# Attention with alternating score pairs, its coefficient on GpSimd, and the output projection begun between the last tiles

## The reference, cut to what matters

```python
def block(qi):
    s = jnp.einsum('bqhmd,bkhmd->bhmqk', qi, k) * scale
    p = jax.nn.softmax(s, axis=-1)
    pd = p[:, :, 0] - lam * p[:, :, 1]
    return jnp.einsum('bhqk,bkhv->bqhv', pd.astype(v.dtype), v)
...
o = _rmsnorm(o, p['subln_g'][l]) * (1.0 - lam_init)
mix = jnp.concatenate([o.reshape(B, S, D_ATTN), rg], axis=-1) @ p['w_out'][l]
```

## Time and profile before

| what | value |
| --- | --- |
| median of three runs | 2250.62 us |
| profiled execution | 2247.88 us, span 2246.1 us |
| TensorE busy | 2166.9 us, 96% of the span |
| VectorE busy | 1552.5 us, 69% |
| ScalarE busy | 834.0 us, 37% |
| GpSimd busy | 47.2 us, 2% |
| attention, first pair of tile 2 to first pair of tile 35 | 1144.97 to 1314.96 us |
| mean granted TensorE clock | 0.991 |

### The profile page before, as it was taken

The page is one execution under the profiler, slowest core; times in us unless marked ns, Lnnn a source line. Parts: engine busy times, 40 slices in busy tenths (PEclk is TensorE's granted clock), DMA queues, the critical chain, the costliest instruction groups (busy, mean ns, idle before and its releaser), DMA issues.

```text
span 2246.1 us, 34066 instructions
## 1 busy us (share of the span) xinstructions
PE 2166.9 (96%) x13144; PEld 2103.6 (94%) x13144; DVE 1552.5 (69%) x2580; ACT 834.0 (37%) x1503; POOL 47.2 (2%) x79
## 2 busy tenths in 40 slices
PE   5999999999999999999989989999999999999997
PEld 4989999999999999899977879899999999999996
DVE  6977777777878775675768874686454547756556
ACT  5622232334212143655267762353232323411122
POOL 0000000000000000000011030000000000000000
PEclk8999999999999999999999999999999999999999
...
## 3 DMA queue, kind: packets, MB, share of 16 engines
...
...
## 4 chain that ended last, share of the span: by engine, by line
PE 89%; DVE 7%; ACT 2%; issue 1%; DMA 1%; SPq 0%; DVEq 0%; ACTq 0%
PE ps L786 16%; PE ps L788 16%; PE ps L787 16%; PE ps L861 9%; PE ps L862 9%; PE ps L863 9%; PE ps L1041 7%; PE ps L1172 2%; DVE sb_nmx L2415 1%; PE ps L1023 1%; PE ps L1117 1%; DMA sb_stage<-in_w_mod 1%; PE ps L1158 1%; PE ps L1125 1%; ACT sb_pr L1677 1%
## 5 line engine op out<-in xcount | busy, mean ns | idle before, releaser
L786 PE MATMUL ps<-sb_hH,sb_wH 128*128 128x384 f32 x1664 | 563.3, 339 | 8.0 <-DVE sb_wL L1906 3.7
L787 PE MATMUL ps<-sb_hL,sb_wH 128*128 128x384 f32 x1664 | 557.9, 335 | 0.0
L788 PE MATMUL ps<-sb_hH,sb_wL 128*128 128x384 f32 x1664 | 557.7, 335 | 0.0
L786 PEld LDWEIGHTS ps<-sb_hH,sb_wH 128*128 128x128 f32 x1664 | 313.9, 189 | 15.2 <-DVE sb_wL L1906 4.4
L787 PEld LDWEIGHTS ps<-sb_hL,sb_wH 128*128 128x128 f32 x1664 | 313.7, 188 | 1.2 <-issue 0.3
L788 PEld LDWEIGHTS ps<-sb_hH,sb_wL 128*128 128x128 f32 x1664 | 313.7, 189 | 0.0
L2180 DVE SCALAR_TENSOR_TENSOR sb_x<-ps,sb_mod,sb_x 128x384 f32<-128x384 f32 (+2 forms) x384 | 186.3, 514 | 172.7 <-PE ps L788 167.4
L861 PE MATMUL ps<-sb_hH,sb_wH 128*128 128x384 f32 x704 | 236.1, 335 | 4.2 <-DVE sb_tmp L2040 3.9
L862 PE MATMUL ps<-sb_hL,sb_wH 128*128 128x384 f32 x704 | 235.9, 335 | 0.0
L863 PE MATMUL ps<-sb_hH,sb_wL 128*128 128x384 f32 x704 | 235.8, 335 | 0.0
L1326 ACT ACTIVATE sb_wH<-sb_wide 128x512 fp32r<-128x512 f32 x176 | 110.9, 633 | 228.8 <-DVE sb_wide L1924 223.7
...
## 6 DMA issues: line engine op xcount, KB each, us to landing
...
```

The lines of the kernel that those rows point to most:

```text
L786: pe.matmul(o, wH, xH, start=begin, stop=False)
L787: pe.matmul(o, wH, xL, start=False, stop=False)
L788: return pe.matmul(o, wL, xH, start=False, stop=end)
```

## The change

Five things are done.

1. The order of the scores of a latent tile: three stacked for m = 0 as before; then three times a pair followed by one stacked matmul for m = 1. The signal that map 0 is complete is still given by the third pair's matmul for m = 0.
2. The coefficient of the difference is computed on GpSimd (`coefficient`, one multiplication by two per-partition scalars). VectorE only makes the reciprocal of the second sum, at the start of the next turn and ahead of the maxima, and the difference waits for `coef_ready`. All 36 coefficients stand in GpSimd's list ahead of the 27 multiplications of the attended tiles.
3. ScalarE no longer scales the attended tile by the reciprocal of the first sum. The norm absorbs it: before the roots, VectorE adds the squared sum times 128 times epsilon (`add_floor`).
4. `SPLIT_AT` has five entries instead of six, later ones; the sixth piece of work (queries of head 1) is done ahead of the loop. Of the three last value matmul groups one moves to turn 0 and two stay in turn 1.
5. At the end, the high parts of the operand tiles of chunk 0 are made in turns 35, 36 and 37 (`MIX_AT`) and the matmuls of `first_mix` stand between the groups of turns 37 and 38.

The core of the diff (left out: declarations and renamed semaphores):

```diff
-MIX_ORDERS = ((0, 1, 2, 4, 5, 6, 7, 3), (4, 5, 6, 7, 0, 1, 2, 3), (4, 5, 6, 7, 0, 1, 2, 3))
+MIX_ORDERS = ((4, 5, 0, 1, 2, 6, 7, 3), (4, 5, 6, 7, 0, 1, 2, 3), (4, 5, 6, 7, 0, 1, 2, 3))
 MIX_ORDER = MIX_ORDERS[1]
-SPLIT_AT = {1: (1, 0), 3: (1, 1), 5: (2, 0), 7: (2, 1), 11: (3, 0), 13: (3, 1)}
+MIX_AT = {TILES - 1: (4, 5), TILES: (0, 1, 2), TILES + 1: (6, 7)}
+SPLIT_AT = {4: (1, 1), 8: (2, 0), 10: (2, 1), 17: (3, 0), 20: (3, 1)}
...
-            sums = sb("sums", [P, 3, 2], F32, s)
-            rec = sb("rec", [P, 6, 2], F32, s)
+            sums = sb("sums", [P, TILES, 2], F32, s)
+            floor = sb("floor", [P, TILES], F32, s)
+            rec = sb("rec", [P, 3], F32, s)
...
-            for hd in range(NH):
-                stack_queries(hd)
-                stack_keys(hd)
+            def coefficient(u):
+
+                r = u % 3
+                pool.wait_ge(coef_ready, 2 * u + 1)
+                pool.tensor_scalar(coef[:, r:r + 1], rec[:, r:r + 1], sums[:, u, 0:1], nlam[:, 0:1], ALU.mult,
+                                   ALU.mult).then_inc(coef_ready, 1)
+
+            stack_queries(0)
+            stack_keys(0)
+            pool.wait_ge(small_in, 3)
+            for u in range(TILES):
+                coefficient(u)
+                if u == 2:
+                    stack_queries(1)
+                elif u in SPLIT_AT:
+                    hd, is_k = SPLIT_AT[u]
+                    (stack_keys if is_k else stack_queries)(hd)
             pool.wait_ge(o_rec, 1)
...
+            def stacked_scores(u, m, begin, spans=range(3)):
 
                 hd, q = u // QT, u % QT
-                for p in range(3):
+                for p in spans:
                     mm = pe.matmul(ps[:, 3 * m + p, 0:CH], queries(hd)[:, m, (q - 1) * P:q * P],
                                    keys_of(hd)[:, m, p * CH:(p + 1) * CH], start=begin, stop=not begin)
                 return mm
...
                 pe.wait_ge(e_done, 2 * u)
                 for p in range(3):
                     mm = low_scores(u, 0, p, False)
+                    if p == 2:
+                        mm.then_inc(s_ready, 1)
                     low_scores(u, 1, p, True)
+                    mm = stacked_scores(u, 1, False, (p,))
                 mm.then_inc(s_ready, 1)
-                stacked_scores(u, 1, False).then_inc(s_ready, 1)
 
             def group(u, g):
 
@@ -1173,16 +1192,30 @@
                     if k == nk - 1:
                         m.then_inc(o_ready, 1)
 
+            def first_mix(f, ks, begin, end):
+                if begin:
+                    pe.wait_ge(raw_used[f], used_wo[f] + 2)
+                for k in ks:
+                    pe.wait_ge(mix_lo, mixed(0, k))
+                    m = three(ps[:, f * NC, 0:CH], wiH[:, f, k * P:(k + 1) * P], wiL[:, f, k * P:(k + 1) * P],
+                              hv(hH, 0, k), hv(hL, 0, k), begin and k == ks[0], end)
+                if end:
+                    m.then_inc(w_ready, 1)
+
             pe.wait_ge(m_ev, 6 + 48)
             pe.wait_ge(acst, N_ACST)
             pe.wait_ge(roped, 1)
-            pe.wait_ge(v_ev, 15)
+            pe.wait_ge(v_ev, 13)
             for u in range(TILES + 3):
+                if u == 1:
+                    pe.wait_ge(v_ev, 15)
                 if u < TILES:
                     scores(u)
-                if u == 1:
-                    for n in range(15, 18):
-                        v_last(n)
+                if u == 0:
+                    v_last(15)
+                elif u == 1:
+                    v_last(16)
+                    v_last(17)
                 elif u == 2:
                     pe.wait_ge(v_ev, 18)
                 for g in range(3):
@@ -1190,9 +1223,16 @@
                         group(u - 2, g)
                     if g < 2 and 0 <= u - 3 < TILES:
                         values(u - 3, g)
+                    if u == TILES + 1 and g < 2:
+                        first_mix(0, (4 + g,), g == 0, False)
                 if u == TILES:
                     for hd in range(NH - 1):
                         outputs(0, hd)
+                elif u == TILES + 1:
+                    first_mix(1, (4, 5), True, False)
+                    first_mix(0, (0, 1, 2), False, False)
+                elif u == TILES + 2:
+                    first_mix(1, (0, 1, 2), False, False)
 
             def out_chunk(i, c, between=None):
 
...
-                pe.wait_ge(raw_used[f], used_wo[f] + 2)
-                first_mix(f, MIX_ORDERS[0][:KT - 1], True, False)
+                first_mix(f, (6, 7), False, False)
...
+                elif n == 12:
+                    qk_high(1, 0)
...
                 if u < TILES:
                     act.wait_ge(mx_ready, 2 * u + m + 1)
                     act.activation(by_bank(probs(u, m)) if u % QT else probs(u, m), unit(u, m), ACT.Exp,
-                                   bias=nmx[:, u % 2, m:m + 1], accum_out=sums[:, u % 3, m:m + 1]).then_inc(e_done, 1)
+                                   bias=nmx[:, u % 2, m:m + 1], accum_out=sums[:, u, m:m + 1]).then_inc(e_done, 1)
 
             def out_squares(u):
 
                 hd, t = u // QT, u % QT
                 act.wait_ge(o_ready, u + 1)
                 act.wait_ge(o_ss, u + 1)
-                act.activation(tmp[:, 3, 0:P], ps[:, 7, 0:P], ACT.Square, scale=rec[:, u % 6, 0:1],
+                act.activation(tmp[:, 3, 0:P], ps[:, 7, 0:P], ACT.Square,
                                accum_out=ss[:, hd, t:t + 1]).then_inc(o_ss, 1)
                 if u == QT:
                     act.wait_ge(outs, 48)
-                act.activation(attended(hd, t), ps[:, 7, 0:P], ACT.Copy, scale=rec[:, u % 6, 0:1]).then_inc(o_done, 1)
+                act.activation(attended(hd, t), ps[:, 7, 0:P], ACT.Copy).then_inc(o_done, 1)
 
             def roots_of_outputs(h0_, h1):
 
-                act.wait_ge(o_ss, 1 + h1 * 9)
-                act.activation(ss[:, h0_:h1], ss[:, h0_:h1], ACT.Sqrt, bias=eps[:, 0:1], scale=1.0 / P).then_inc(o_sd, 1)
+                act.wait_ge(o_floor, h1 // NH + 1)
+                act.activation(ss[:, h0_:h1], ss[:, h0_:h1], ACT.Sqrt, scale=1.0 / P).then_inc(o_sd, 1)
 
             def mix_high(c, k):
 
-                if (c, k) == (0, 0):
+                if (c, k) == (0, 4):
+                    act.wait_ge(t_ready, groups_before(TILES - 2))
+                elif (c, k) == (0, 6):
                     act.wait_ge(t_ready, groups_before(TILES - 1))
                 elif (c, k) == (1, 4):
                     act.wait_ge(o_done, TILES)
@@ -1710,17 +1743,16 @@
                 p_copy(u - 2, 0)
                 exps(u, 0)
                 exps(u, 1)
-                if u == 1:
-                    for n in range(15, 18):
+                if u < 2:
+                    for n in ((15,), (16, 17))[u]:
                         v_evac(n)
                 if u in SPLIT_AT:
                     qk_high(*SPLIT_AT[u])
                 p_copy(u - 2, 2)
                 if 3 <= u < TILES + 3:
                     out_squares(u - 3)
-                if u == TILES:
-                    for k in MIX_ORDERS[0][:KT - 1]:
-                        mix_high(0, k)
+                for k in MIX_AT.get(u, ()):
+                    mix_high(0, k)
                 if u == (NH - 1) * QT + 4:
                     roots_of_outputs(0, NH - 1)
                 if (NH - 1) * QT + 5 <= u < (NH - 1) * QT + 7:
...
                 dve.tensor_reduce(nmx[:, u % 2, m:m + 1], unit(u, m), AX.XY if u % QT else AX.X, ALU.max,
                                   negate=True).then_inc(mx_ready, 1)
 
-            def difference(u):
+            def add_floor(h0_, h1):
+
+                at = slice(h0_ * QT, h1 * QT)
+                dve.wait_ge(o_ss, 1 + h1 * QT)
+                link(dve.scalar_tensor_tensor(floor[:, at], sums[:, at, 0], P * EPS, sums[:, at, 0], ALU.mult, ALU.mult))
+                dve.tensor_tensor(ssf[:, at], ssf[:, at], floor[:, at], ALU.add).then_inc(o_floor, 1)
+
+            def reciprocal(u):
 
                 r = u % 3
                 dve.wait_ge(e_done, 2 * u + 2)
-                link(dve.reciprocal(rec[:, u % 6], sums[:, r]))
-                link(dve.scalar_tensor_tensor(coef[:, r:r + 1], sums[:, r, 0:1], nlam[:, 0:1],
-                                              rec[:, u % 6, 1:2], ALU.mult, ALU.mult))
-                dve.scalar_tensor_tensor(probs(u, 0), probs(u, 1), coef[:, r:r + 1], probs(u, 0), ALU.mult,
+                dve.reciprocal(rec[:, r:r + 1], sums[:, u, 1:2]).then_inc(coef_ready, 1)
+
+            def difference(u):
+
+                dve.wait_ge(coef_ready, 2 * u + 2)
+                dve.scalar_tensor_tensor(probs(u, 0), probs(u, 1), coef[:, u % 3:u % 3 + 1], probs(u, 0), ALU.mult,
                                          ALU.add).then_inc(pd_ready, 1)
 
             def p_copy(u):
@@ -2443,6 +2485,8 @@
                 m.then_inc(mix_lo, 1)
 
             for u in range(TILES + 3):
+                if 1 <= u <= TILES:
```

(15 more changed lines are left out.)

24 lines of the change are left out of this document (9 added, 15 removed).

## The result

The kernel with the change takes **2290.76 us**, the median of four executions (2286.25 to 2293.82). The kernel before takes 2249.42 us. The ratio is 1.0186, with a 95% interval of 1.0161 to 1.0211: it is 1.9% slower, just under the 2% that the prediction named as what tells from no change, with the interval's upper end just above it. One execution of the kernel before (2699.86 us) and one of e7 (4677.85 us) lie far outside all others and count in no ratio. The forecast was 2276 us, within 2256 to 2292.

A forecast was written before the change was run, and what follows sets the result against it. A loop over TensorE, VectorE and ScalarE bounds each latent tile at 4.97 us. Terms 24.8 + 2.5 + 1.2 - 2.2 + 0 = +26.3 on 2247.9 gave 2274 us profiled, 2277 median; stated 2276, range 2256 to 2292.

The forecast's parts named there:

- No change beyond 2%: Whole kernel: the time stays within 2% (45 us) of before, 2205.6 to 2295.6 us; chance 0.90.
- The lone piece: Scores on TensorE: a pair or stacked matmul alone between two mode changes takes 0.38 us, bounds 0.17 and 0.44.
- The loop: Latent tile over three engines: first pair to maxima grows from 0.83 to 2.00 us, the tile from 4.97 to 6.14.
- the rival that VectorE is the true bound: Latent tiles: VectorE's own list sets the pace, 4.70 us a tile, 2235 us in all; chance 0.05.
- The rival of a free change: Scores on TensorE: alternating mode changes cost nothing, 5.32 us a tile, 2254 us in all; chance 0.10.
- TensorE's own 0.83: Scores of a latent tile: TensorE's own work grows by 0.83 us to 5.80 a tile, within 6.14.
- Coefficient, low parts, tables: Attention loop: moved coefficient worth nothing, low parts hidden; ScalarE's two table loads ahead of tile 32 cost 0.8 us.
- Context tiles, +2.5: Steps around the three context tiles: TensorE works without pause, so its 0.83 us counts each time, +2.5 us.
- The other 27 steps: Steps between latent tiles, tile 2 to tile 35: 27 x 6.14 plus 0.8 for tables against 141.8, +24.8 us.
- The start, -2.2: Start of the attention: value matmuls of turn 0 fill TensorE's gaps and the clock may stay up, -2.2 us (-3.6 to +1).
- The clock: Attention: TensorE's clock falls to its lower level, up to 1.7 us each, past 2% from 11 falls; chance 0.06.
- The end, 0: Attention's end and first output chunk: 3 to 4 us won, as much lost waiting for GpSimd; 0 (-4 to +5).

The follow-up runs named there:

- e7: Kernel before with one stacked matmul of map 1 moved behind the first pair, one alternation instead of two: 2267.85 us, ratio 1.0076.
- e1: Kernel before with only the new order of the scores: 2285.06 us, ratio 1.0165.
- e6: Kernel before with the third pair's matmul for map 1 split off behind one stacked matmul, map 0 complete as early as before: 2263.71 us, ratio 1.0067.
- e2: Changed kernel with the old order of the scores, the rest of the change kept: 2249.35 us, ratio 1.0004.
- e9: Changed kernel run once more without any edit: 2288.16 us, ratio 1.0177 to the kernel before.
- e11: e5 with twelve matmuls that nobody reads added in turn 2: 2239.12 us, ratio 0.9956 to the kernel before.
- e10: e4 with twelve more matmuls that nobody reads in turn 2: 2284.34 us, ratio 1.0159 to the kernel before.
- e4: Changed kernel with nine matmuls that nobody reads ahead of each context tile's values: 2285.01 us, ratio 1.0169 to the kernel before.
- e8: Changed kernel, new order kept, with GpSimd's nine multiplications of chunk 0 moved behind the coefficients of tiles 32 to 34: 2284.98 us, ratio 1.0166.
- e5: Changed kernel with the old order and GpSimd's nine multiplications of chunk 0 moved behind the coefficients of tiles 32 to 34: 2241.66 us, ratio 0.9970.

## Why the prediction was right

**No change beyond 2%, and the range: both held, both narrowly; the number was 15 us low.** In the profiled execution the forecast was 2247.9 + 26.3 = 2274.2 us and 2293.82 were measured, 19.6 more. The median of 2290.76 lies 1.2 us below the upper end of the range. That end was made of a lone piece of 0.44 us and an end of +5, which did not come; the clock, which the range was said to leave out in the main, used up their room. The mechanism of the loop was right, but that the range held is in part luck. Of the signs named for a wrong forecast one came, a clock below 1.00 in the middle of the attention; the others (starts 0.17 apart, a tile below 5.5 us, differences waiting for GpSimd) did not.

**The lone piece, 0.38 us: right.** 0.37 to 0.38 from start to start in the after profile, in e1 and in e7. That 0.10 lies on each side of a change was read from two neighbours in the earlier trace rows; e6 and e7, which add one alternation in two different places, both give 0.57 for it, that is 0.20 for each change added to the 0.17 of the matmul.

The weight load of a lone pair in the after profile:

```profile
1178.97 0.19 PEld L1142 LDWEIGHTS ps<-sb_kstack,sb_qk_rest 64*128 64x128 f32 x2 [0.19 <-issue]
```

**The loop, 0.83 to 2.00 and the tile 4.97 to 6.14: right.** 1.97, and 6.11 to 6.12. The rest of the loop, 2.66 + 1.48, did not move by 0.01. e2 excludes the rival that VectorE is the true bound: relieved of its 0.45 us it idles 0.48. The rival of a free change falls with every start in the alternation. Nor is a weight load pulled ahead across a change: in the row above it starts with its matmuls, at 1178.97, after the weight loads have stood idle for 0.19 us, and those of the stacked matmuls on either side do the same; the load of the transposes behind them, in one mode with its neighbour, starts at 1180.23, 0.15 us ahead of its matmul. The Trainium skill, "TensorE: Matmul & The Clock Gate", section "The mechanism", which says that a load aimed at the background buffer is pulled ahead of running matmuls, is not borne out in this place. With its page "TensorEngine Tiling (Array Packing)", section "Key Properties", by which a change of the tiling mode drains TensorE, the trace agrees, by 0.20 us a change.

**TensorE's own 0.83, called within 6.14: right here, and closer than it looked.** Measured 0.80. e6 shows that half a microsecond of it alone, with nothing added ahead of the maxima, already sets the tile, through ScalarE's copy. The prediction compared TensorE's list alone and did not see this second loop. In the changed kernel it is 2.15 + 0.52 + 0.39 + 1.22 + 1.48 = 5.76 us, 0.35 less than 6.11: the sum came out because the first loop grew more.

**Coefficient, low parts, tables, nothing or 0.8: right.** The coefficient takes 0.34 us on GpSimd and is ready long before it is needed; steps between latent tiles with a low part are no longer than others, 6.12; the step with the two tables takes 7.04, 0.92 more.

**Context tiles, +2.5: too small.** The changed table places the high parts of turns 8 and 17 on ScalarE just ahead of the context tiles 9 and 18, and the prediction gave them no price. ScalarE in turn 8 and TensorE at the start of turn 9, in e9 and at the full clock:

```profile
1189.15 1.04 ACT L1674 ACTIVATE sb_qk_split<-sb_x 128x1024 fp32r<-128x1024 f32 x1
```

```profile
1190.72 0.52 PE L1177 MATMUL ps<-sb_ident,sb_pr 128*128 128x128 f32 x3 [0.93 <-ACT sb_pT L1701]
```

The high part stands ahead of the copy for which TensorE's next transposes wait, 0.93 us. From the first pair of tile 8 to that of tile 10, and from 17 to 19, it is 11.2 us, around tile 27 with no high part 10.25; before, the three took 9.68, 9.42 and 9.41. The old order with the same table shows it too: 10.05, 10.04 and 9.10 in e11. That is +4.1 instead of +2.5. The other 27 steps give +24.1 in e10, where +24.8 was forecast. The two misses have opposite signs: together +28.2 with the clock up, where +27.3 was forecast.

**The start, -2.2: right**, -2.6 in the after profile.

**The clock: the term that was mis-sized.** The sum held none; the falls stood in a rival of their own at 0.06. The prediction's argument against it was that steps with a low part left gaps of 1.2 us and kept 1.00 in the earlier trace rows. Those were the wrong steps: the falls came after the long wait of turn 2 (2.31 us) and at the turns behind the context tiles. Four falls in the after profile's steps, two in e9's, none in e10's. A fall also cost more than the 1.7 us that the rival gave it: the lower level lasted 17.1, 10.3, 10.3 and 6.8 us there, so four falls cost 16 us, where the rival needed eleven for its 2%. The after profile against e10 gives 214.33 - 198.2 = 16.1 us for 44.4 us, e9 205.52 - 198.2 = 7.3 us for 23.9, e9 against after 8.8 for 20.5, e4 less its 1.2 us of filling 5.2 for 13.7, e8 10.9 for 34.1: 0.3 to 0.4 us for each microsecond at the lower level, less than the half microsecond that TensorE's own work loses. I take the rest to be hidden by its waits in the loop; no run shows that apart. Of the 19.6 us that the forecast was short of the profile, 16.1 are this. Behind turn 2 it is the wait that counts: all eleven profiled executions whose kernel leaves it empty show a fall there, of 3.4 to 17.1 us, and the two that fill it, e10 and e11, none. What decides in one execution whether the clock falls behind a context tile, I did not find: e9 and the after profile are the same there until the fall.

**The end, 0: right in kind, mis-sized.** Forecast were 3 to 4 us won and 3 to 4 us of waiting for GpSimd. Won were 3.7 us (e5's tail of 24.27 against 27.96), as forecast. Lost by GpSimd's queue were 7.7 (e2's 31.93 against e5's 24.27), about twice the forecast: in the after profile 4.44 us of waiting, and 6.8 us at the lower clock behind it. The tail grew by 4.1, of which 1.2 were named, so the term is +2.9, inside the -4 to +5 given. e5 and e8 undo the cause alone: -7.7 and -6.6 us. Nine multiplications took 7.6 us, between 5.3 and 11.8.

Together: 16.1 for the clock, 2.9 for the end, 28.2 - 27.3 = 0.9 for the steps and -0.4 for the start are 19.5 of the 19.6 us. The 16.1 and the 0.9 both rest on the estimate of 198.2 us; their sum does not.
